# Gate and up projections by Strassen's seven block products, down products in a stage of their own

## The chip, the cores and the metric

The kernel runs on one core of one Trainium2 chip. The metric is the device time of the core in microseconds (us); a single matmul is told in nanoseconds (ns). TensorE does the matmuls, ScalarE (ACT), VectorE (DVE) and GpSimd (POOL) the elementwise work, and SyncE (SP) issues nearly all DMAs. Each engine runs its own instructions strictly in the order in which the program lists them, and engines wait for each other on semaphores.

## The reference

One layer of a streaming encoder on 1152 rows (1024 prompt rows and 8 sample streams of 16 rows), width 1024. Two recurrent mixers come first, then their output product with the residual, then a feed-forward network with a causal convolution of three taps over the rows, which holds most of the arithmetic:

```
x = x + concat(o_gla, o_mlstm) @ w_out
h = rmsnorm(x)                                    # 1152 x 1024
g = h @ w_g ; u = h @ w_u                         # 1024 -> 2816 each
gc = conv_b + sum(conv_w[j] * gp[:, j:j + L] for j in range(3))   # gp: g with the carried rows before it
x = x + (gelu(gc) * u) @ w_d                      # 2816 -> 1024
y = rmsnorm(x)
```

All values are float32. Every large product is made of three matmuls: each operand x is split into a rounded part hi and the rest lo = x - hi, and hi*hi + lo*hi + hi*lo is summed in PSUM.

## The kernel before

The program has three parts that follow each other on every engine: `front` (norm, input projections, GLA mixer), `back` (mLSTM mixer, output product, residual, second norm) and `ffn`. The change leaves `front` as it is.

`back` lists its work once, in `back_order`, and each engine walks that list and does its own share of every item, so an item's place in the list is its place in the queue of each engine. A step s handles 128 rows, in the order `M_STEPS` = 8, 0, 1, ..., 7. Its items are `num` and `um` (recurrence), `turn_b` (hidden rows transposed by TensorE, taken from PSUM by ACT as hi and by DVE as lo), `b` (the second half of the output product, added to the residual rows by DVE, L2041), `sum` (squares on ACT, root on POOL) and `scaled` (ACT scales the 128 rows into `n_rows`, L1755). `turn_n` transposes a block of 384 scaled rows (L1894, 48 transposes) and writes h2T hi (ACT, L1765) and lo (DVE, L2007); the last block of 384 is turned at the head of `ffn` (L2247, 24 transposes). Outputs in PSUM go through a ring of 8 banks: the n-th output waits until the one 8 before it was taken.

`ffn` goes over 11 pairs of 128-wide tiles f of the 2816 columns, nine of the pairs in a hardware loop. For each tile of a pair and each of three blocks of 384 rows (`RBW`) TensorE makes the gate and the up product, 8 parts of the depth by 3 matmuls of 384 columns each (`up`). ACT copies the gate to `gate_prompt` (L2194), DVE does the convolution (L2321, L2324, L2328), ACT the gelu (L2208), DVE multiplies with the up product (L2335), ACT and POOL split the result (L2210, L2161). Then the same pair's down products follow: for 9 row tiles and 2 halves, 2 tiles f by 3 matmuls of 512 columns into bank 6 or 7, added to the residual rows `m_x` in SBUF by DVE (L2341). Weights come in pieces of 128x1024 (512 KB) through three slots, are rounded by ACT (L2172) and their rest made by POOL (L2151). The residual never leaves SBUF. After the last down product DVE and ACT finish the rows (L2232, L2353, L2360) and SP stores them (L2139).

Of the kernel before, what the change touches and what calls it, by code (L numbers as in the profile page):

```python
# [97 lines left out]
class Turn:  # L98

    def __init__(self, nc, sem, name, hT, ident, gain, banks, source, spread=None, eight=None):
        self.spread, self.eight = spread, eight
        self.hT, self.ident, self.gain, self.banks, self.source = hT, ident, gain, banks, source
        self.nb = len(banks)
        self.turned, self.hi_done, self.lo_done = (sem(f"{name}_{n}") for n in ("turned", "hi", "lo"))

    def bank_of(self, rb, k):
        return self.eight[k] if rb == self.spread else self.banks[(rb * KD + k) % self.nb]

    def pe_turn(self, pe, rb, ks=range(KD)):
        for k in ks:
            n = rb * KD + k
            if rb == self.spread:
                if rb and k == 0:
                    pe.wait_ge(self.lo_done, n)
            elif n >= self.nb:
                pe.wait_ge(self.lo_done, n - self.nb + 1)
            for j in range(JR):
                t = pe.transpose(self.bank_of(rb, k)[:, j * P:(j + 1) * P], self.source(rb, j, k), self.ident)  # L120
            t.then_inc(self.turned, 1)

    def act_hi(self, act, rb, ks=range(KD)):
        for k in ks:
            n = rb * KD + k
            act.wait_ge(self.turned, n + 1)
            act.activation(self.hT[0][:, k, rb * RBW:(rb + 1) * RBW], self.bank_of(rb, k)[:, 0:RBW], ACT.Copy,
                           scale=self.gain[:, k:k + 1]).then_inc(self.hi_done, 1)

    def dve_lo(self, dve, rb, ks=range(KD)):  # L130
        for k in ks:
            n = rb * KD + k
            s = slice(rb * RBW, (rb + 1) * RBW)
            dve.wait_ge(self.hi_done, n + 1)
            dve.scalar_tensor_tensor(out=self.hT[1][:, k, s], in0=self.bank_of(rb, k)[:, 0:RBW],
                                     scalar=self.gain[:, k:k + 1], in1=self.hT[0][:, k, s].bitcast(F32),
                                     op0=ALU.mult, op1=ALU.subtract).then_inc(self.lo_done, 1)


class Norm(Turn):  # L140

    def __init__(self, nc, ctx, sem, name, rows, scaled, squares, hT, ident, gain, banks, **spread):
        sb = lambda n, s: ctx.enter_context(nc.sbuf_tensor(f"{name}_{n}", s, F32))
        self.rows, self.scaled_rows, self.squares = rows, scaled, squares
        self.ss = sb("sumsq", [P, RT])
        self.inv = sb("inv", [P, RT])
        self.rstd = sb("rstd", [P, RT])
        self.summed, self.inverted, self.rooted, self.scaled = (  # L150
            sem(f"{name}_{n}") for n in ("summed", "inverted", "rooted", "scaled"))
        super().__init__(nc, sem, name, hT, ident, gain, banks,
                         lambda rb, j, k: scaled(rb * JR + j)[:, k * P:(k + 1) * P], **spread)

    def pe_turn(self, pe, rb, ks=range(KD)):
        if ks[0] == 0:
            pe.wait_ge(self.scaled, rb * JR + JR)
        super().pe_turn(pe, rb, ks)

    def act_sums(self, act, rb, ready, js=range(JR)):  # L160
        for r in (rb * JR + j for j in js):
            ready(act, r)
            if r:
                act.wait_ge(self.summed, r)
            act.activation(self.squares, self.rows(r), ACT.Square,
                           accum_out=self.ss[:, r:r + 1]).then_inc(self.summed, 1)

    def act_root(self, act, rb):
        act.wait_ge(self.inverted, rb + 1)
        s = slice(rb * JR, rb * JR + JR)  # L170
        act.activation(self.rstd[:, s], self.inv[:, s], ACT.Sqrt).then_inc(self.rooted, 1)

    def dve_invert(self, dve, rb, chain):
        s = slice(rb * JR, rb * JR + JR)
        dve.wait_ge(self.summed, rb * JR + JR)
        chain.link(dve.tensor_scalar(self.ss[:, s], self.ss[:, s], 1.0 / D, EPS, ALU.mult, ALU.add))
        dve.reciprocal(self.inv[:, s], self.ss[:, s]).then_inc(self.inverted, 1)

    def dve_scale(self, dve, rb):
        dve.wait_ge(self.rooted, rb + 1)  # L180
        if rb:
            dve.wait_ge(self.turned, rb * KD)
        for j in range(JR):
            r = rb * JR + j
            dve.tensor_scalar(self.scaled_rows(r), self.rows(r), self.rstd[:, r:r + 1], None,
                              ALU.mult).then_inc(self.scaled, 1)
# [2287 lines left out]
```

## Time and profile before

| | us |
|---|---|
| median of 3 runs | 1436.87 (1436.09 to 1437.58) |
| span of the profiled execution | 1438.3 |
| TensorE busy | 1411.8 (98%) |
| VectorE, ScalarE, GpSimd busy | 602.8, 418.9, 469.9 |
| mean DMA rate over the span | 85 GB/s |

The profiled execution's span is 1.4 us above the median of the timed runs. The busy row shows which engine has idle time at all; the view of waits shows who makes TensorE wait; the chain of work that ended last is by its own line TensorE for 94% of the span. In the 40 slices of the page TensorE is at 9 tenths or more in all but the first and the last:

```
PE   7999999999999999999999999999999999999997
DVE  4444132456743455554242433343333333343437
ACT  5341232343323145741212122221212121303123
POOL 5131343457633244432322323232313131313210
```

### The profile page before, as it was taken

How to read it: one execution, taken by the hardware profiler on the slowest of the kernel's cores; microseconds unless marked ns; L12 is line 12 of the kernel's file. 1: busy time of each engine (PE TensorE's matmuls, PEld its weight loads, DVE VectorE, ACT ScalarE, POOL GpSimd, SP SyncE). 2: the span in 40 equal slices, each digit the busy share in tenths (PEclk: the TensorE clock that was granted, in tenths of full speed). 3: DMA queues.
4: the chain of work that ended last, by engine and by line, in shares of the span. 5: the costliest groups of instructions: out<-in, count | busy, mean ns of one | idle time of the engine just before them, and what ended most of it. 6: DMA issues, size and time to landing. Idle time of an engine off the chain costs nothing.

```text
span 1438.3 us, 22509 instructions
## 1 busy us (share of the span) xinstructions
PE 1411.8 (98%) x8739; PEld 1292.4 (90%) x8739; DVE 602.8 (42%) x1234; ACT 418.9 (29%) x889; POOL 469.9 (33%) x452
## 2 busy tenths in 40 slices
PE   7999999999999999999999999999999999999997
PEld 6988888889997788898989899999999999999895
DVE  4444132456743455554242433343333333343437
ACT  5341232343323145741212122221212121303123
POOL 5131343457633244432322323232313131313210
PEclk9999999999999999999999999999999999999999
DMA  6222632335347573121110101010101010111003
GB/s 238 69 79 81 213 121 86 131 108 164 119 137 268 167 218 104 37 90 50 30 59 29 58 29 58 29 58 29 58 27 60 15 54 33 44 43 44 15 21 131
DMA packets 69472, 122.58 MB, mean 85 GB/s; under 512 B 5607, under 2 KB 41219, under 8 KB 68895
## 3 DMA queue, kind: packets, MB, share of 16 engines
q1 hardware_dynamic: 69263, 121.62, 25.4%
q8 instruction: 44, 0.72, 0.2%
q14 instruction: 21, 0.17, 0.0%
q10 hardware_dynamic: 144, 0.07, 0.0%
HBM read 93.02 MB, written 28.64 MB: 85 GB/s over the span
## 4 chain that ended last, share of the span: by engine, by line
PE 94%; DVE 2%; DMA 1%; ACT 1%; POOL 1%; issue 0%; SPq 0%; POOLq 0%; DVEq 0%; ACTq 0%
PE bank L93 29%; PE bank L95 29%; PE bank L94 29%; PE bank L1874 1%; PE bank L1086 1%; PE bank L1143 1%; DVE m_x L2360 1%; PE bank L1827 1%; DMA m_t_in<-scratch_pT 1%; PE bank L1161 1%; PE bank L1857 0%; PE bank L1886 0%; DVE m_x L2341 0%; PE bank L1856 0%; PE bank L1149 0%
## 5 line engine op out<-in xcount | busy, mean ns | idle before, releaser
L93 PE MATMUL bank<-f_h2T_hi,w_hi 128*128 128x384 f32 x1056 | 354.2, 335 | 0.0
L95 PE MATMUL bank<-f_h2T_hi,w_lo 128*128 128x384 f32 x1056 | 353.9, 335 | 0.0
L94 PE MATMUL bank<-f_h2T_lo,w_hi 128*128 128x384 f32 x1056 | 353.5, 335 | 0.0
L2161 POOL TENSOR_TENSOR f_a_lo<-f_gate_conv,f_a_hi 128x384 fp32r<-128x384 f32 x66 | 67.2, 1017 | 574.0 <-ACT f_a_hi L2210 574.0
L93 PEld LDWEIGHTS bank<-f_h2T_hi,w_hi 128*128 128x128 f32 x1056 | 198.3, 188 | 0.4
L94 PEld LDWEIGHTS bank<-f_h2T_lo,w_hi 128*128 128x128 f32 x1056 | 198.2, 188 | 0.4
L95 PEld LDWEIGHTS bank<-f_h2T_hi,w_lo 128*128 128x128 f32 x1056 | 198.2, 188 | 0.0
L2341 DVE TENSOR_TENSOR m_x<-bank,m_x 128x512 f32<-128x512 f32 x198 | 136.9, 692 | 126.1 <-PE bank L95 126.1
L93 PE MATMUL bank<-w_hi,f_a_hi 128*128 128x512 f32 x396 | 154.4, 390 | 0.4 <-DVE m_x L2341 0.2
L95 PE MATMUL bank<-w_hi,f_a_lo 128*128 128x512 f32 x396 | 154.3, 390 | 0.0
L94 PE MATMUL bank<-w_lo,f_a_hi 128*128 128x512 f32 x396 | 154.3, 390 | 0.0
L2321 DVE TENSOR_SCALAR f_gate_conv<-f_gate_prompt,f_taps 128x384 f32<-128x384 f32 (+1 forms) x66 | 35.7, 541 | 271.8 <-ACT f_gate_prompt L2194 179.4
L791 POOL TENSOR_TENSOR w_lo<-w_raw,w_hi 128x1024 fp32r<-128x1024 f32 x33 | 81.1, 2472 | 132.5 <-ACT w_hi L868 132.4
L2194 ACT ACTIVATE f_gate_prompt<-bank 128x384 f32<-128x384 f32 x44 | 21.7, 493 | 331.6 <-PE bank L95 331.6
L93 PE MATMUL bank<-w_hi,p_h1T_hi 128*128 128x512 f32 x288 | 113.0, 392 | 1.0 <-POOL w_lo L791 1.0
L95 PE MATMUL bank<-w_hi,p_h1T_lo 128*128 128x512 f32 x288 | 112.2, 390 | 0.0
L94 PE MATMUL bank<-w_lo,p_h1T_hi 128*128 128x512 f32 x288 | 112.1, 389 | 0.0
L93 PE MATMUL bank<-p_h1T_hi,w_hi 128*128 128x384 f32 x312 | 108.5, 348 | 3.1 <-DVE p_h1T_lo L1219 2.8
L94 PE MATMUL bank<-p_h1T_lo,w_hi 128*128 128x384 f32 x312 | 106.1, 340 | 0.0
L95 PE MATMUL bank<-p_h1T_hi,w_lo 128*128 128x384 f32 x312 | 106.1, 340 | 0.0
L2151 POOL TENSOR_TENSOR w_lo<-w_raw,w_hi 128x1024 fp32r<-128x1024 f32 x42 | 100.5, 2392 | 4.9 <-ACT w_hi L2172 4.9
L93 PEld LDWEIGHTS bank<-w_hi,f_a_hi 128*128 128x128 f32 x396 | 74.3, 188 | 16.8 <-DVE m_x L2341 1.1
(240 smaller groups left out, 2118.7 us busy)
## 6 DMA issues: line engine op xcount, KB each, us to landing
w_raw<-in_w SPq DMA_DIRECT2D x82, 512.0 KB, 3.6
f_raw<-in_w SPq DMA_DIRECT2D x21, 512.0 KB, 3.5
scratch_pN<-p_n_out SPq DMA_DIRECT2D x36, 256.0 KB, 2.1
scratch_pT<-p_t_out SPq DMA_DIRECT2D x36, 192.0 KB, 1.9
p_arena<-in_x SPq DMA_DIRECT2D x9, 512.0 KB, 5.9
p_arena<-scratch_pN SPq DMA_DIRECT2D x18, 256.0 KB, 3.3
m_x<-in_x SPq DMA_DIRECT2D x9, 512.0 KB, 7.9
m_t_in<-scratch_pT SPq DMA_DIRECT2D x9, 512.0 KB, 7.2
```

Of the source, the lines that this page charges most:

```text
L93: pe.matmul(out, stat[0], mov[0], start=start, stop=False)
L94: pe.matmul(out, stat[0], mov[1], start=False, stop=False)
L95: return pe.matmul(out, stat[1], mov[0], start=False, stop=stop)
L791: pool.tensor_tensor(w_lo[:, i % NS_, :], raw[:, i % 2, :], w_hi[:, i % NS_, :].bitcast(F32), ALU.subtract).then_inc(g["piece_split"], 1)
L1086: mm = pe.matmul(out[c * HP:(c + 1) * HP, e, j * 2 * P + at:j * 2 * P + at + QP], half(kx, e)[:, n, j * P + c * HP:j * P + (c + 1) * HP], ...
L1143: mm = pe.matmul(dst(2 * j + e), gsc[:, 2 * j + e, :], vs(2 * j + e), start=True, stop=True, skip_group_check=True)
L1161: mm = pe.matmul(half(out, h)[:, at:at + P], kdn[r, b % 2, j, (h % 2) * DK:(h % 2 + 1) * DK], vin[r, s % 2, h * P:(h + 1) * P], start=True ...
L2151: pool.tensor_tensor(w_lo[:, unit, :], slots[slot], w_hi[:, unit, :].bitcast(F32), ALU.subtract).then_inc(piece_split, 1)
L2161: pool.tensor_tensor(a_lo[q][:, s], gc[:, n % 2, :], a_hi[q][:, s].bitcast(F32), ALU.subtract).then_inc(a_split, 1)
L2194: act.activation(gp[:, 2 + rb * RBW:2 + (rb + 1) * RBW], g[:, 0:RBW], ACT.Copy).then_inc(g_out, 1)
L2321: ins = dve.tensor_scalar(dst, src(2), tap[2], tap[3], ALU.mult, ALU.add)
L2341: dve.tensor_tensor(x, bank[6 + half], x, ALU.add).then_inc(down_added, 1)
```

## The change

The rows are cut into two parts p: rows 0 to 639 as two blocks of 320, rows 640 to 1151 as two blocks of 256. The depth of 1024 and the pair (gate columns, up columns) of a tile f are cut in two as well, and each 2x2 block product is made by seven products in place of eight. One of the seven has a depth of 4 parts, so 4 x 3 = 12 matmuls of 320 or 256 columns. A product needs a sum of weight blocks (a `unit`, 128x512, seven for each f) and a sum of row blocks (a `half`, 4x320 or 4x256 columns on 128 partitions, seven for each p), each split in hi and lo. Outputs accumulate in three PSUM groups, with partial values moved to SBUF in between.

`back` now scales the residual rows in place (after a copy was stored in DRAM, `scratch_res`), transposes them 128 rows at a time (`turn_n`, 8 transposes), and works off the first row and weight sums from its list. `gate_up` makes all products of the 22 tiles without a hardware loop and stores the activations in DRAM (`scratch_act`, 22 x 576 KB). `down` loads them, the down weights and the residual rows again, and makes the down products in 11 chunks of two tiles, with all 8 banks in turn. Matmuls of the down products, their DVE adds and the finishing of the rows keep their number and shape.

```diff
-RBW = 384 row blocks, 24 matmuls of 384 columns for each of gate and up
+NP2 = (320, 256)
+QUADS = 2 * NF
+HALF_POOL = [(0, 0), (0, 1), (0, 2), (1, 0), (1, 1), (1, 4), (1, 5)]
+HALF_DVE = [(0, 3), (0, 4), (0, 5), (0, 6), (1, 2), (1, 3), (1, 6)]
+def quad_order():
+    order = [(0, 0), (0, 1)]
+    for t in range(QUADS):
+        order += [(t, 2), (t, 3), (t, 4)]
+        order += [(t + 1, 0), (t + 1, 1)] if t + 1 < QUADS else []
+        order += [(t, 5), (t, 6)]
...
 back_order, around the last two steps:
+        order += [("turn_n", 4), ("t", 0, 0), ("t", 0, 1), ("half", 0, 0), ("unit", 5)] if s == RT - 1 else []
         order += [("b", s - 2, 1), ("sum", s - 2, 1)] if s >= 2 else take(1)
+        order += {..., 8: [("half", 0, 1), ("unit", 6)]}.get(s, [])
         order += [("b", s - 1, 0)] if s else take(1)
         order += [("sum", s - 1, 0)] if s else []
+        order += {..., 8: [("t", 0, 2), ("scaled", 8), ("scaled", 5), ("half", 0, 2)]}.get(s, [])
+    order += [("b", RT - 2, 1), ("turn_b", RT - 1), ("sum", RT - 2, 1), ("turn_n", 8), ("t", 0, 3)]
+    order += [("b", RT - 1, 0), ("half", 0, 3), ("turn_n", 5), ("b", RT - 1, 1), ("scaled", 6), ("sum", RT - 1, 0), ("sum", RT - 1, 1)]
...
 gate_up, SP:
+        for t in range(QUADS):
+            if t % 2 == 0 and t // 2 + 1 < NF:
+                half.load(sp, a, t // 2 + 1)
+            if t:
+                store(t - 1)
+        store(QUADS - 1)
+        sp.wait_ge(tails_done, 2 * NF)
+        sp.dma_start(o["conv"], tails[:, :, :]).then_inc(tails_out, 16)
 gate_up, ACT (t is a tile f of one part p):
+        for t in range(QUADS):
+            if t:
+                copy_u2(t); copy_p7(t); [keep_tails(f - 1)]; gelu(t - 1); [load_cache(f)]
+            if t == 1:
+                half.hi(act, (1, 5)); half.hi(act, (1, 6))
+            if t + 1 < QUADS:
+                copy_p1(t + 1)           # waits for multiply(t - 1)
+            if t == 0:
+                half.hi(act, (1, 4)); units(7, 8)
+            elif t == 1:
+                units(8, 14)
+            else: units of f + 1: three after p = 0, four after p = 1
+        keep_tails(NF - 1)
+        gelu(QUADS - 1)
 gate_up, DVE:
+        for t in range(QUADS):
+            take_c22(t); [plus(f + 1, 2), plus(f + 1, 3)]
+            take_up1(t + 1); [plus(f + 1, 0), plus(f + 1, 1)]
+            take_c21(t); conv(t)
+            if t == 0:
+                half.lo(dve, (1, 6))
+            multiply(t)
 down, SP, behind all of the above:
+        done.made(sp, last - 1, 3)
+        load_w(0)
+        done.made(sp, last - 1, 5)
+        load_w(1)
+        load_a(0); load_a(1)
+        ... residual rows 0 to 8, then load_w(f), load_a(f) for f = 2 to 21
```

TensorE's waits in `product(t, j)`: j = 2 for `copy_p1(t)`, 4 for `copy_u2(t)`, 5 for `take_c22(t)`, 6 for `copy_p7(t)`, each for its unit (POOL's `unit_lo`), and at f = 0 for its half. The first down matmul waits for the hi and lo of weight tile 0 (ACT, then POOL) and of activation tile 0 (ACT, then DVE).

## Rows read from the trace of the kernel before

**Rows 1.** The page: span and busy time of each engine.

```profile
span 1438.3 us, 22509 instructions
PE 1411.8 (98%) x8739; PEld 1292.4 (90%) x8739; DVE 602.8 (42%) x1234; ACT 418.9 (29%) x889; POOL 469.9 (33%) x452
```

**Rows 2.** Stretches: us, busy by engine, granted clock, DMA share, GB/s.

```profile
5.00:10.00 5.00, 2.08 (x10) 2.12 (x11) 1.51 (x2) 4.28 (x7) 3.11 (x6) 1.00 1.03 408
15.00:20.00 5.00, 5.00 (x16) 5.00 (x17) 3.39 (x7) 4.91 (x9) 1.83 (x2) 0.50 1.00 389
712.00:1400.00 688.00, 688.00 (x3660) 649.74 (x3659) 247.46 (x441) 147.01 (x298) 184.03 (x110) 1.00 0.12 40
```

**Rows 3.** TensorE over time: start us, us, operation; matmul pitch by width.

```profile
567.12 1.05 PE L1827 MATMUL bank<-m_t_in 128*128 128x128 f32 x8
567.93 0.48 PE L93 MATMUL bank<-w_hi,m_mix_b_hi 128*128 128x512 f32 x1
...
577.09 1.47 PE L1894 MATMUL bank<-ident,n_rows 128*128 128x128 f32 x12
578.39 1.06 PE L1827 MATMUL bank<-m_t_in 128*128 128x128 f32 x8
...
603.85 0.33 PE L93 MATMUL bank<-f_h2T_hi,w_hi 128*128 128x384 f32 x1
...
663.44 0.39 PE L93 MATMUL bank<-w_hi,f_a_hi 128*128 128x512 f32 x1
680.44 0.39 PE L93 MATMUL bank<-w_hi,f_a_hi 128*128 128x512 f32 x1
...
1000.04 0.33 PE L93 MATMUL bank<-f_h2T_hi,w_hi 128*128 128x384 f32 x1
1004.20 0.33 PE L93 MATMUL bank<-f_h2T_hi,w_hi 128*128 128x384 f32 x1
...
1428.45 0.39 PE L95 MATMUL bank<-w_hi,f_a_lo 128*128 128x512 f32 x1
```

**Rows 4.** TensorE at the half clock, matmuls of 384 columns.

```profile
18.84 0.52 PE L93 MATMUL bank<-p_h1T_hi,w_hi 128*128 128x384 f32 x1
19.16 0.52 PE L94 MATMUL bank<-p_h1T_lo,w_hi 128*128 128x384 f32 x1
```

**Rows 5.** VectorE, ScalarE, GpSimd groups by shape: busy us, mean ns, idle before.

```profile
L2341 DVE TENSOR_TENSOR m_x<-bank,m_x 128x512 f32<-128x512 f32 x198 | 136.9, 692 | 126.1 <-PE bank L95 126.1
L2324 DVE SCALAR_TENSOR_TENSOR f_gate_conv<-f_gate_prompt,f_taps,f_gate_conv 128x384 f32<-128x384 f32 x44 | 27.2, 618 | 3.8 <-DVE f_gate_conv L2321 2.9
L2360 DVE SCALAR_TENSOR_TENSOR m_x<-m_x,f_rstd,w_raw 128x1024 f32<-128x1024 f32 x9 | 11.4, 1272 | 0.3 <-ACT f_rstd L2224 0.3
L2172 ACT ACTIVATE w_hi<-w_raw 128x1024 fp32r<-128x1024 f32 x42 | 43.9, 1044 | 0.0
L2210 ACT ACTIVATE f_a_hi<-f_gate_conv 128x384 fp32r<-128x384 f32 x66 | 34.7, 526 | 96.5 <-DVE f_gate_conv L2335 96.5
L2151 POOL TENSOR_TENSOR w_lo<-w_raw,w_hi 128x1024 fp32r<-128x1024 f32 x42 | 100.5, 2392 | 4.9 <-ACT w_hi L2172 4.9
L1649 POOL TENSOR_TENSOR m_wt<-m_wt,m_caus 128x512 f32<-128x512 f32 x9 | 11.5, 1280 | 5.3 <-DMA m_wq<-scratch_rows 5.3
```

**Rows 6.** VectorE and GpSimd over time, around 105 us: start us, us, operation.

```profile
104.35 2.54 DVE L1256 TENSOR_TENSOR_SCAN p_arena<-p_arena 4x1152 f32<-4x1152 f32 x1
104.61 4.48 POOL L791 TENSOR_TENSOR w_lo<-w_raw,w_hi 128x1024 fp32r<-128x1024 f32 x1 [4.97 <-ACT w_hi L868]
106.93 3.23 DVE L1258 TENSOR_TENSOR p_arena<-p_arena 4x1024 f32<-4x1024 f32 x1
```

**Rows 7.** From the last output products to the feed-forward part, over time.

```profile
587.76 1.13 DVE L1965 SCALAR_TENSOR_TENSOR m_hidden<-bank,m_den,m_o_in 128x128 f32<-128x128 f32 x4
...
594.69 0.60 PE L1886 MATMUL bank<-ident,m_hidden 128*128 128x128 f32 x4
595.32 0.69 ACT L1793 ACTIVATE m_mix_b_hi<-bank,cols 128x512 fp32r<-128x512 f32 x1
596.05 0.75 DVE L2030 SCALAR_TENSOR_TENSOR m_mix_b_lo<-bank,cols,m_mix_b_hi 128x512 fp32r<-128x512 f32 x1 [0.47 <-ACT m_mix_b_hi L1793]
596.94 0.47 PE L93 MATMUL bank<-w_hi,m_mix_b_hi 128*128 128x512 f32 x1
620.33 1.28 ACT L2208 ACT_TABLE_LOAD   x1
```

**Rows 8.** SyncE's queue at the end of the kernel, over time.

```profile
1374.39 0.34 SPq L2134 DMA_DIRECT2D w_raw<-in_norm_f  x1
1399.93 0.34 SPq L2136 DMA_DIRECT2D out_conv<-f_tails  x1
1413.44 20.59 SPq L2139 DMA_DIRECT2D out_y<-m_x  x9
```

**Rows 9.** DMA issues of the page: KB each, median us from issue to landing.

```profile
w_raw<-in_w SPq DMA_DIRECT2D x82, 512.0 KB, 3.6
p_arena<-in_x SPq DMA_DIRECT2D x9, 512.0 KB, 5.9
```

More of the change, by code:

```diff
@@ L95, in mm3 @@
     return pe.matmul(out, stat[1], mov[0], start=False, stop=stop)
[L98 to L137, printed above, removed]
@@ L140 @@
[L140 to L186, printed above, removed]
@@ L1488, in back_order @@
         order += [("mask", s + 1)] if s + 1 < RT else []
-        order += [("turn_b", s - 1), ("scaled", 3), ("ffn", 0)] if s == RT - 1 else []
+        order += [("turn_b", s - 1), ("unit", 4)] if s == RT - 1 else []
         order += [("num", s)]
@@ L1520, in back_entries @@
         elif x[0] == "turn_n":
-            out += [(("turn_n", x[1], k), "dve") for k in TURN_HALVES[x[2]]]
+            out += [(x + (i,), "dve") for i in range(2)]
         elif x[0] in ("num", "um"):
@@ L1524, in back_entries, with back @@
     return out
-def back(nc, a, o, mem, rows_n, halves_n, early, late, done, ident, cols, col_m, col_d, ssq, ssn, rstd2, power, w, raw, bank,
-         sem, block):
+def back(nc, a, o, mem, early, half, done, ident, cols, col_m, col_d, ssq, ssn, rstd2, power, w, raw, bank, sem, block):
     order = back_order()
@@ L2166, in _ @@
[L2166 removed]
+        for x in HALF_POOL:
+            if x[0] == 1:
+                half.lo(pool, x)
+        for n in range(7, 7 * NF):
+            half.unit_lo(pool, n)
     @block.scalar
     def _(act):
[L2170 to L2178 removed]
@@ new lines, in keep_tails, with units @@
+        def keep_tails(f):
+            act.wait_ge(c21_done, 2 * f + 2)
+            act.activation(tails[:, f, 0:2], gp[:, PROMPT:PROMPT + 2], ACT.Copy).then_inc(tails_done, 1)
+            act.activation(tails[:, f, 2:2 + 2 * NB].rearrange("p (b e) -> p b e", e=2), gs[:, :, LB:SX],
+                           ACT.Copy).then_inc(tails_done, 1)
+        def units(first, end):
+            for n in range(first, min(end, 7 * NF)):
+                half.unit_hi(act, n)
+        half.hi(act, (0, 4))
@@ L2289, in _ @@
-        pairs(pe, body)
+        n = 0
+        for fs in DOWN_CHUNKS:
+            for r in range(RT):
+                for side in range(2):
+                    out = bank[DOWN_BANKS[n % 8]]
+                    if n < 8:
+                        done.bank_free(pe, DOWN_BANKS[n])
+                    else:
+                        added.wait(pe, n - 7)
+                    for f in fs:
+                        if r == 0 and side == 0:
+                            w_split.wait(pe, f + 1)
+                            a_split.wait(pe, f + 1)
+                        mm = mm3(pe, out, [y[:, r * P:(r + 1) * P] for y in rows(f)],
+                                 [y[:, side * 512:(side + 1) * 512] for y in weights(f)], f == fs[0], f == fs[-1])
+                    mm.then_inc(filled.sem, 1)
+                    n += 1
```

1018 lines of the change are left out of this document (655 added, 363 removed).

## The prediction

> **What bounds the kernel now.** I read the page's busy times first: TensorE is busy for 1411.8 of 1438.3 us, no other engine for half of it [rows 1]. The stretches come next. From 712 to 1400 us TensorE is busy for all of 688 us at the full clock [rows 2], so the feed-forward part is bound by the pitch of its matmuls alone. The timeline gives this pitch. From 1000.04 to 1004.20 us there are 24 starts of 384 columns, 173.3 ns each; from 663.44 to 680.44 there are 75 of 512 columns, 226.7 ns each [rows 3]. The difference, 53.4 ns for 128 columns, is 128 cycles of 2.4 GHz, so the pitch is N/2.4 + 13.3 ns. Eight matmuls of 128 columns take 0.81 us, 101 ns each [rows 3], more than the 66.6 ns of that formula: below some width another limit of about 101 to 112 ns takes over (112 if the last of the eight is left out of the count: 1.05 us less the 0.27 of one, over 7). The part from the first gate matmul (603.85) to the last down matmul (1428.45) is 3168 x 173.3 = 549.0 us of gate and up, 1188 x 226.7 = 269.3 of down, 24 transposes of 108 ns (twelve in 1.30 us, same group) = 2.6, and 3.7 us of small stalls.
>
> **What is saved for sure.** Gate and up become 22 x 7 x 12 = 1848 matmuls of 320 and 1848 of 256 columns. By the formula these take 146.7 and 120.0 ns: 271.1 + 221.8 = 492.9 us, 56.1 less than 549.0. The nearest rows from below and above are 128 columns (101 to 112 ns) and 384 (173.3). 256 columns stay above the floor of the first, so I take the line through the two wide rows. If a floor adds to it, 5 ns on the 256-wide ones cost 9 us; I see no way to be faster than the line. The down products stay at 269.3 us. The 72 transposes stay too, 8 of them move ahead of the first product. So TensorE alone would bring 1438.3 - 56.1 = 1382.2 us. The rest of this part is what stands against it, and all of it is idle time of TensorE at three places that the trace of before doesn't have.
>
> A rule on the pitch speaks for a little more: the Trainium skill, page "TensorE: Matmul & The Clock Gate", section "Back-to-back issue gap", gives N/2.4 + 2.5 ns. By it the saving would be 3168 x 162.5 - 1848 x (135.8 + 109.2) ns = 62 us; the trace has 173.3 and not 162.5 ns at 384 columns, and the trace decides.
>
> **Prices of the new elementwise work.** DVE takes 692 ns for 512 columns, 618 for 384 from SBUF, 1272 for 1024: about 1.04 ns a column and 0.2 us; 1280 columns cost 1.5 us, 640 cost 0.9. ACT takes 1.04 us for 1024 and 0.53 for 384, so 1.27 for 1280 and 0.6 for 512. POOL takes 1.28 us for 512 and 2.39 for 1024, so 2.95 for 1280 [rows 5]. One thing more decides: DVE and POOL exclude each other when a DVE instruction has two SBUF inputs. At 104.61 us POOL's split, 2.39 us elsewhere, takes 4.48, since DVE's scan runs until 106.89; then DVE's next operation starts at 106.93 and lasts 3.23 us, until POOL is through at 109.09 and 1.07 us more [rows 6]. They take turns. Nearly all new DVE work (plus, row sums, halves, convolution) has two SBUF inputs. By that row each such operation behind a running POOL one waits for its rest. The Trainium skill has this on the page "SBUF — State Buffer", section "Who interferes with whom": two SBUF inputs on DVE against a GpSimd read lock each other out for whole instructions; this trace agrees.
>
> **Place 1, the last steps of back.** TensorE's b(8,0) needs the last turn_b: in before TensorE ends it at 595.29, ACT and DVE take 0.69 + 0.75 us, and b starts at 596.94 [rows 7]. Now ACT has in front of it, in list order, half (0,0), unit 5, sum (6,1), half (0,1), unit 6, sum (7,0), scaled 8, scaled 5, half (0,2). Sum (6,1) waits for DVE's add b(6,1), which stands behind turn_n 4 (2 x 0.69) and two row sums of 1.5 us, one of them behind POOL's 2.95 us split. I count from the end of hidden(8) on DVE, in before 588.85 [rows 7], now some 1.5 us later behind two weight sums and a turned block, 590.3: states 1.1, turn_n 1.3, sums 3.0, add 0.7 = 596.4. ACT then: 0.7 + 1.27 + 0.6 + 0.7 + 1.14 + 1.14 + 1.27 + 0.7 for turn_b = 603.9, DVE 0.75: b(8,0) starts at 604.9, where TensorE, with 8 more transposes ahead of it than before (0.9 us behind 596.94), is ready at 597.8. That is 7.1 us, and up to 10.8 with POOL's turn in between and its norm chain behind. I take 9.
>
> **Place 2, the first two tiles.** ACT's copy_p1(2) waits for multiply(0). Unit 8, which TensorE's (2,1) needs, stands behind copy_p1(2). From the end of product (0,6): c21 0.5, conv 2.5, table load 1.28 [rows 7], gelu 0.74, halves (1,5) and (1,6) on ACT 2.1, lo (1,6) on DVE 1.3, multiply 0.5, copy 0.45, unit 0.6 + 1.28 = 11.3 us. TensorE has in that time (1,2), (1,3), (1,4) at 1.44 and (2,0) at 1.76 = 6.1. So it idles for 5.2 us at least. DVE is late besides: between (0,4) and conv(0) it has three row sums and three halves of 1.3 to 1.5 us and a fourth sum, while POOL splits three halves of 2.4 us against them. With turns taken I count 10 us more; so 5 to 16, and I take 13.
>
> **Place 3, between gate_up and down.** SP's queue keeps its order: in before norm_f, conv and y leave one after the other, each behind its wait [rows 8]. So load_w(0) stands behind store(43), which waits for the last multiply, although its own wait is long satisfied. After the last gate matmul: c21 0.6, conv 2.5, gelu 0.7, multiply 1.0, so the store leaves at 4.9 us and the first weights at 5.8. A lone piece lands 3.6 us after issue, nine in a burst 5.9 [rows 9], at 408 GB/s [rows 2], 1.3 us for each 512 KB: w0 at 10.4, w1 11.7, a0 13.2, a1 14.6. Then ACT a1 hi to 16.6 and POOL's and DVE's split of w1 and a1 to 19.2, with f = 0's three matmuls done meanwhile: 18.6 us, 15 if the bytes flow better. I take 18. Later loads are covered: a chunk is 108 x 226.7 ns = 24.5 us for 2.2 MB, and eight banks let TensorE run 8 outputs (10.9 us) ahead of DVE.
>
> **The clock.** At 15 to 20 us, after TensorE had waited much, the granted clock was 0.50, 1.2 GHz [rows 2], and 384 columns took 320 ns [rows 4]. Each of the three idle stretches can bring that back: 5 us at half the clock lose about 2.3. I take 6 for three, 0 to 9.
>
> **Steady state and end, costed at nothing.** A tile f takes 12 x 7 x (146.7 + 120.0) = 22.4 us of TensorE. POOL has 7 x 1.28 = 9.0, ACT about 9, DVE about 13, of which 9 exclude POOL. The tightest wait is (t,5) for take_c22(t), behind conv, gelu and multiply of t-1; with POOL's units in between I count it 0.7 to 0.9 us ahead of TensorE. Matmuls, adds and finishing of the last chunk are the same as before.
>
> **The sum.** 1438.3 - 56.1 + 9 + 13 + 18 + 6 = 1428.2 us of span; the timed median lies 1.4 below the span, so 1426.8, rounded to 1427. Low: 7 + 5 + 15 + 0 gives 1407.8. High: 11 + 16 + 20 + 9 gives 1436.8, with 9 us for the 256-wide floor 1446.
>
> **The rivals.** (a) The start is hidden (chance 0.17): ACT and DVE get their work into gaps and places 1 and 2 cost under 10 together, place 3 stays. 1438.3 - 56.1 + 7 + 18 + 2 - 1.4 = 1408. For it speaks that DVE is under half busy [rows 1]; against it, that the waits are in list order. (b) Slower: the turn-taking of DVE and POOL makes take_c22 late in each tile. Price: if conv meets two POOL units of 1.28 us more than I counted, 2.6 - 0.8 = 1.8 us a tile, x 22 = 40, 1467; one in every other part, 0.5 us, 1438. It decides from 0.5 us a tile on. Rows 6 show the mechanism; that my count leaves 0.8 us speaks against it. Chance 0.22. (c) The saving is not as said: a floor of weight loads brings 256 columns to 125 ns, 1436. Chance 0.08. (d) My forecast, 0.53.
>
> **How the numbers follow.** The measurement tells some 0.2%, 2.9 us, from no change: faster is under 1434, slower above 1439.7. Rival (a) and nearly nine tenths of (d) are faster, together 0.63; the rest of (d), most of (c) and the near edge of (b) are within, 0.15; the others are slower, 0.22. The range takes (a)'s middle and cuts off (b)'s far end: 1406 to 1446.
>
> **What would show it.** Pitches of 146 to 148 and 119 to 121 ns in the timeline; gate and up end to end near 493 us plus 13; idle TensorE ahead of b(8,0) behind ACT's m_mix_b hi; ahead of (2,1) behind POOL's unit; ahead of the first down matmul some 18 us behind DMA and the splits, with w_raw's first down load issued after the last store; clock 0.5 after each. I am wrong if TensorE waits for DVE in every tile, or if the three places sum to under 25 or over 55 us.

## The result and the profile after

The changed kernel takes 1433.9 us (median of 17, 1430.42 to 1437.78), the kernel before, measured beside it, 1437.44 (17 runs, 1436.09 to 1442.18). The ratio is 0.9971, 95% interval 0.9962 to 0.9979: 3.5 us faster where I forecast 10. In every one of these runs the span is 1.8 to 1.9 us shorter than the time.

Some lines of the page of the changed kernel; they answer to [rows 1]:

```profile
span 1430.9 us, 23368 instructions
PE 1367.8 (96%) x9267; PEld 1238.5 (87%) x9267; DVE 824.6 (58%) x1463; ACT 470.2 (33%) x967; POOL 538.0 (38%) x503
PE   7999999999999999779999999999999499999997
PEclk9999999999999999898999999999999799999998
```

TensorE is busy 44 us less, not 56, and two dents have come, at slices 17 to 18 and 32. What ended TensorE's waits (total, times, longest):

```profile
PE bank L93 <- DVE d_a_lo L2650: 17.1, 2, 15.3
PE bank L110 <- POOL w_lo L298: 6.8, 1, 6.8
PE bank L330 <- ACT m_x L1710: 3.9, 1, 3.9
PE bank L93 <- DVE m_mix_b_lo L2168: 3.8, 1, 3.8
PE bank L110 <- POOL f_units L298: 2.5, 1, 2.5
PE bank L110 <- ACT f_u L2282: 1.2, 1, 1.2
```

These are the three places of the prediction: place 1 is 3.9 + 3.8 = 7.7 us, place 2 is 6.8 + 2.5 + 1.2 and two waits of 1.0 = 12.5, place 3 is 17.1, 37.3 together against 9 + 13 + 18 = 40. One more wait of 1.0 us, for DVE's take_c22 in the last tile at 1121 us, belongs to none of them. The stretches (busy, count, then granted clock, DMA share, GB/s), which answer to [rows 2]:

```profile
596.00:610.00 14.00, 8.99 (x34) 7.18 (x35) 9.69 (x8) 7.57 (x12) 11.71 (x10) 0.63 0.10 39
640.00:657.00 17.00, 10.82 (x48) 10.48 (x49) 8.84 (x10) 3.66 (x7) 11.50 (x8) 0.60 0.11 34
657.00:1110.00 453.00, 453.00 (x3404) 453.00 (x3404) 300.67 (x490) 160.31 (x366) 187.15 (x140) 1.00 0.22 73
1127.00:1150.00 23.00, 8.66 (x25) 6.50 (x26) 7.38 (x9) 4.85 (x5) 4.92 (x2) 0.56 0.90 343
1200.00:1400.00 200.00, 200.00 (x860) 161.03 (x859) 123.38 (x159) 25.80 (x24) 33.09 (x12) 1.00 0.16 60
```

From 657 to 1110 us TensorE is busy for all of 453.00 us: the steady state has no wait. The clock is 0.56 to 0.63 at the three places and 1.00 in the two long stretches. The last line holds the surprise: 200 us with 860 matmuls of 512 columns are 232.6 ns each, at full clock with TensorE always busy. The timeline of TensorE (start us, us), for the pitches, which answers to [rows 3]:

```profile
699.95 0.29 PE L110 MATMUL bank<-f_b_hi,w_hi 128*128 128x256 f32 x1
701.14 0.28 PE L111 MATMUL bank<-f_t_lo,f_units 128*128 128x256 f32 x1
...
703.49 0.31 PE L110 MATMUL bank<-f_t_hi,w_hi 128*128 128x320 f32 x1
705.40 0.31 PE L111 MATMUL bank<-w_lo,w_hi 128*128 128x320 f32 x1
...
1199.67 0.39 PE L94 MATMUL bank<-w_lo,d_a_hi 128*128 128x512 f32 x1
1201.07 0.39 PE L94 MATMUL bank<-w_lo,d_a_hi 128*128 128x512 f32 x1
```

A step is the time from one start to the next. 10 steps of 256 columns in 1.19 us are 119 ns, 13 of 320 in 1.91 are 147 (forecast 120.0 and 146.7), 6 of 512 in 1.40 are 233.3 ns. In the kernel before the last were 226.7 [rows 3].

Place 1, ScalarE ahead of b(8,0), against [rows 7]. It is ACT's list, as predicted: scaled 5, half (0,2) and turn_b follow each other without a pause.

```profile
598.80 1.15 ACT L1710 ACTIVATE m_x<-m_x,rstd 128x1024 f32<-128x1024 f32 x1 [1.65 <-POOL rstd L1858]
599.86 1.25 ACT L396 ACTIVATE f_t_hi<-ra_k 128x1280 fp32r<-128x1280 f32 x1
601.02 0.67 ACT L1938 ACTIVATE m_mix_b_hi<-bank,cols 128x512 fp32r<-128x512 f32 x1
602.61 0.77 PE L93 MATMUL bank<-w_hi,m_mix_b_hi 128*128 128x512 f32 x1 [3.81 <-DVE m_mix_b_lo L2168]
```

Place 2, TensorE, GpSimd and ScalarE:

```profile
639.01 2.35 POOL L402 TENSOR_TENSOR f_b_lo<-rb_k,f_b_hi 128x1024 fp32r<-128x1024 f32 x1 [5.87 <-ACT f_b_hi L396]
641.31 2.24 POOL L298 TENSOR_TENSOR w_lo<-w_raw,w_hi 128x512 fp32r<-128x512 f32 x1
643.70 0.61 PE L110 MATMUL bank<-f_b_hi,w_hi 128*128 128x320 f32 x1 [6.85 <-POOL w_lo L298]
647.28 0.44 ACT L2266 ACTIVATE f_up<-bank 128x320 f32<-128x320 f32 x1 [7.40 <-PE bank L112]
649.72 0.61 PE L110 MATMUL bank<-f_b_hi,f_units 128*128 128x320 f32 x1 [2.48 <-POOL f_units L298]
```

Here (2,0) is the product j = 0 of t = 2. I had the longest wait one product too late. It is (2,0)'s, for unit 7: POOL splits half (1,5) first, and that half stands behind the first gelu. copy_p1(2) then waits for (2,0) itself, and unit 8 stands behind it. Unit 7 takes 2.24 us, beside a DVE split that runs until 642.43, where the next unit, at 648.31, takes 1.27: the taking of turns of [rows 6], as the Trainium skill's page "SBUF — State Buffer", section "Who interferes with whom", has it.

Place 3, SyncE's queue, which answers to [rows 8], and the first down matmul; w0 is issued 0.8 us behind the last store:

```profile
1128.88 0.32 SPq L2232 DMA_DIRECT2D scratch_act<-c_lo  x1
1129.72 0.94 SPq L2558 DMA_DIRECT2D e_w_lo<-in_w  x2
1139.53 0.77 PE L93 MATMUL bank<-d_w_hi,d_a_hi 128*128 128x512 f32 x1 [15.29 <-DVE d_a_lo L2650]
```

Two profiles are compared best from a point that both have. An a product is the first half of the output product, the matmuls with m_mix_a. The first of back starts at 441.68 us in the profile of before and at 438.78 in that of after, although nothing ahead of it differs; over all fourteen profiles it lies between 438.3 and 442.4. From there to the end before takes 996.6 us, after 992.1. Below, "from the first a product" is this number.

### The profile page after: what moved, and what is told of

It is laid out like the page before. It is cut to its first block, busy times and chain, and to the rows that moved or that the text cites. A ratio compares the mean times of both kernels' runs of the same rounds, so it can differ in the third digit from the quotient of the medians.

```text
span 1430.9 us, 23368 instructions
## 1 busy us (share of the span) xinstructions
PE 1367.8 (96%) x9267; PEld 1238.5 (87%) x9267; DVE 824.6 (58%) x1463; ACT 470.2 (33%) x967; POOL 538.0 (38%) x503
## 3 DMA queue, kind: packets, MB, share of 16 engines
q1 hardware_dynamic: 81359, 157.01, 31.7%
## 4 chain that ended last, share of the span: by engine, by line
PE 90%; DVE 3%; DMA 2%; POOL 2%; ACT 2%; issue 1%; SPq 0%; DVEq 0%; ACTq 0%; POOLq 0%
PE bank L93 17%; PE bank L95 16%; PE bank L94 16%; PE bank L110 11%; PE bank L112 11%; PE bank L111 11%; PE bank L2016 1%; PE bank L1213 1%; PE bank L1270 1%; PE bank L1969 1%; DMA m_t_in<-scratch_pT 1%; PE bank L1288 1%; POOL f_b_lo L402 0%; PE bank L1999 0%; PE bank L1140 0%
## 5 line engine op out<-in xcount | busy, mean ns | idle before, releaser
L2680 DVE TENSOR_TENSOR d_x<-bank,d_x 128x512 f32<-128x512 f32 x198 | 134.8, 688 | 97.3 <-PE bank L95 96.8
L110 PE MATMUL bank<-f_t_hi,w_hi 128*128 128x256 f32 (+1 forms) x412 | 121.3, 294 | 1.2 <-ACT f_u L2282 1.2
L111 PE MATMUL bank<-f_t_lo,w_hi 128*128 128x256 f32 (+1 forms) x412 | 121.1, 294 | 0.0
L112 PE MATMUL bank<-f_t_hi,w_lo 128*128 128x256 f32 (+1 forms) x412 | 121.0, 294 | 0.0
L110 PE MATMUL bank<-f_b_hi,w_hi 128*128 128x320 f32 (+1 forms) x360 | 107.8, 299 | 8.8 <-POOL w_lo L298 6.8
L94 PE MATMUL bank<-w_lo,d_a_hi 128*128 128x512 f32 x288 | 113.9, 395 | 0.0
L95 PE MATMUL bank<-w_hi,d_a_lo 128*128 128x512 f32 x288 | 113.8, 395 | 0.0
L93 PE MATMUL bank<-w_hi,d_a_hi 128*128 128x512 f32 x288 | 113.6, 394 | 0.0
L111 PE MATMUL bank<-f_b_lo,w_hi 128*128 128x320 f32 (+1 forms) x360 | 107.4, 298 | 0.0
L112 PE MATMUL bank<-f_b_hi,w_lo 128*128 128x320 f32 (+1 forms) x360 | 107.4, 298 | 0.0
```

What stands on the lines that cost most here:

```text
L93: pe.matmul(out, stat[0], mov[0], start=start, stop=False)
L94: pe.matmul(out, stat[0], mov[1], start=False, stop=False)
L95: return pe.matmul(out, stat[1], mov[0], start=False, stop=stop)
L110: pe.matmul(out, stat[0], mov[0], start=start, stop=False, skip_group_check=True)
L111: pe.matmul(out, stat[0], mov[1], start=False, stop=False, skip_group_check=True)
L112: return pe.matmul(out, stat[1], mov[0], start=False, stop=stop, skip_group_check=True)
```

## The experiments

Two questions are open: why a down matmul takes 6.5 ns more, and what each of the three places and the clock is worth.

**The pitch: banks and waits, or where the tiles lie.** Four runs. two_banks:

```diff
-DOWN_BANKS = (7, 3, 5, 4, 2, 0, 6, 1)
+DOWN_BANKS = (7, 6) * 4
...
-                        added.wait(pe, n - 7)
+                        added.wait(pe, n - 1)
```

> The changed kernel, but with the down products going in turn to banks 7 and 6 only and each waiting for the add of the output two before, as in the kernel before. In the changed kernel a 512-column matmul of the down stage takes 233.3 ns (232.2 in the chunks of f = 0, 1; 8, 9; 16, 17), in the kernel before 226.8. Theory A (the place of the operands in SBUF: the a tiles begin 320 or 0 bytes past a multiple of 512, the w tiles 352): the pitch stays at 233.3, idle time between outputs stays near 0. Rival B (eight banks in turn, or a TensorE queue that is never held up by a wait, makes the matmuls slower): the pitch falls to 226.8, and the down stage gets 7 us shorter.

Measured: 1451.66 us (one run). The pitch stays; here in the chunk of f = 8, 9, 13 steps in 3.02 us, 232.3 ns (233.1 over the whole stage without the waits):

```profile
1259.96 0.39 PE L95 MATMUL bank<-d_w_hi,d_a_lo 128*128 128x512 f32 x1
1262.98 0.39 PE L93 MATMUL bank<-d_w_hi,d_a_hi 128*128 128x512 f32 x1
```

So B falls. The idle time did not stay near 0, though: with two banks TensorE stops whenever DVE puts a split ahead of an add, 11.8 us in eight waits named for the adds, and 824 matmuls in 200 us instead of 860. The eight banks of the change are worth some 18 us (one run).

all_352:

```diff
-        ("inv", [P, RT], F32), ("rstd", [P, RT], F32), ("gap0", [P, 2632], F32),
-        *a(1), *a(2), *a(3), *a(4), *a(5), ("gap1", [P, 688], F32), *wd(0), *wd(1), *a(0), *a(6), *a(7)])
+        ("inv", [P, RT], F32), ("rstd", [P, RT], F32), ("gap0", [P, 2640], F32),
+        *a(1), *a(2), *a(3), *a(4), *a(5), ("gap1", [P, 768], F32), *wd(0), *wd(1), *a(0), *a(6), *a(7)])
```

> The changed kernel, the down stage's tiles moved so that each begins 352 bytes past a multiple of 512, as w_hi and w_lo do (the a tiles by 32 bytes, w0, w1, a0, a6 and a7 by 352). No instruction differs otherwise. Theory A (SBUF place): 512 columns take 226.7 ns in all eleven chunks, 1188 x 6.4 = 7.6 us less, 1426.3 us against 1433.9 for the changed kernel. Rival B (banks and waits) and rival C (other engines' or DMA traffic in the stage): 233.3 ns, 1434, no change.

Measured: 1425.41 us (1424.64 to 1429.49), ratio to before 0.9927 (0.9913 to 0.994); 984.6 us from the first a product, 7.5 less than after. The stretch from 1200 to 1400 us has 884 matmuls, 226.2 ns each, where after has 860:

```profile
1200.00:1400.00 200.00, 200.00 (x884) 165.68 (x883) 127.68 (x168) 29.50 (x31) 31.76 (x12) 1.00 0.15 57
```

before_320 turns it round, on the kernel before:

```diff
-        *hi_lo("a0", [P, ROWS]), ("raw", [P, PIECE], F32), ("gate_conv", [P, 2, RBW], F32),
+        ("gap4", [P, 8], F32), *hi_lo("a0", [P, ROWS]), ("raw", [P, PIECE], F32), ("gate_conv", [P, 2, RBW], F32),
-        ("taps", [P, NF, 4], F32), ("tails", [P, NF, 2 + 2 * NB], F32), ("gap2", [P, 56], F32),
+        ("taps", [P, NF, 4], F32), ("tails", [P, NF, 2 + 2 * NB], F32), ("gap2", [P, 64], F32),
...
```

> The kernel before, its a0 and a1 tiles (the stationary operand of the down products) moved by 32 bytes, from 352 to 384 past a multiple of 512, the weights left at 352. Theory A: its down matmuls go from 226.8 to about 233.3 ns, 1188 x 6.5 = 7.7 us more, about 1445 against 1437.4, while gate and up stay at 173.3 ns. Rivals B and C: 226.8 ns and no change.

The gaps behind a0 and a1 are 8 smaller, so only raw, gate_conv and four small tiles next to a0 move along, none of them an operand of a matmul. The name of the run says 320, the tiles lie at 384. Measured: 1443.93 us (1442.76 to 1446.59), ratio 1.0046 (1.003 to 1.0061): 6.7 us more. One pair's down stage, 108 matmuls, first and last, 107 steps in 24.96 us, 233.3 ns:

```profile
1183.41 0.39 PE L93 MATMUL bank<-w_hi,f_a_hi 128*128 128x512 f32 x1
1208.37 0.40 PE L95 MATMUL bank<-w_hi,f_a_lo 128*128 128x512 f32 x1
```

part_352 moves a1 to a5 alone (gap0 to 2640, gap1 to 680):

> The changed kernel, only the tiles a1 to a5 of the down stage moved by 32 bytes, to 352 past a multiple of 512; w0, w1, a0, a6 and a7 stay at 0, w_hi and w_lo are at 352. It has all four cases in one run: both at 352 (chunks of f = 2, 3; 4, 5; 10, 11; 12, 13; 18, 19; 20, 21), stationary at 0 with weights at 352 (6, 7; 14, 15), both at 0 (f = 0, 8, 16), stationary at 352 with weights at 0 (f = 1, 9, 17). If the stationary operand's place alone decides: 226.7 ns in the first and the last case, 233 in the other two. If both must be odd multiples of 32 bytes: 226.7 in the first case alone. If they must only agree: 226.7 in the first and the third, which the changed kernel's 232.2 (both at 0 or 320) speaks against.

Measured, step means by chunk: 226.7 to 226.8 ns where both operands lie at 352; 233.4 with the stationary one at 0 and the weights at 352; 231.8 to 231.9 in the chunks that mix both at 0 (f = 0, 8, 16; about 231.6 by themselves) with 352 and 0 (f = 1, 9, 17; about 232.1). The stationary tile's place alone doesn't decide, nor does mere agreement. Of these cases only both at 352 is fast. Time 1428.34 us (one run), 988.2 us from the first a product. The cause of the 6.5 ns is thus shown to be the place of the operands in SBUF; the rule behind it isn't, as the last run but one shows.

**Place 3.** early_down moves four loads (w0, w1, a0, a1), four roundings and two splits ahead of the last two stores, the last gelu and the last convolution:

```diff
...
+            if t == QUADS - 1:
+                start.loads(sp)
             if t:
                 store(t - 1)
...
+        start.his(act)
         keep_tails(NF - 1)
         gelu(QUADS - 1)
...
             take_c21(t)
+            if t == QUADS - 1:
+                start.splits(dve)
             conv(t)
...
```

> The changed kernel; SP issues the loads of w0, w1, a0 and a1 ahead of the stores of the last two tiles, ACT rounds them ahead of the last gelu, DVE splits a0 and a1 ahead of the last convolution. Theory (place 3 is the order of SP's queue): the first down matmul starts about 3 us after the last gate matmul instead of 15.3 and the 1.8 us behind it goes, and with less idle time the half clock of 1127 to 1148 us goes or shortens, 2.6 us more: 14 to 17 us less, about 1418. Rival (the bytes or the splits are the limit whatever the order): the four pieces land about as late after their issue as before, 5 to 7 us, and TensorE still waits 8 us or more, about 1426; or the second chunk comes late (its loads wait for the last store) and TensorE waits there.

Measured: 1431.34 us (1429.3 to 1433.62), ratio 0.9959 (0.9944 to 0.9975), far from 1418. The 17.1 us shrank to 2.9, and a new wait came 20 us later (waits of TensorE, then SyncE's queue, then DVE and ACT ahead of the new wait):

```profile
PE bank L93 <- DVE d_x L2713: 8.8, 1, 8.8
PE bank L93 <- DVE d_a_lo L2560: 2.9, 2, 2.6
...
1135.57 0.32 SPq L2233 DMA_DIRECT2D scratch_act<-c_lo  x1
1136.41 5.08 SPq L2605 DMA_DIRECT2D d_x<-scratch_res  x9
...
1155.69 2.07 DVE L2685 TENSOR_TENSOR d_a_lo<-e_a_lo,d_a_hi 128x1152 fp32r<-128x1152 f32 x1 [11.51 <-ACT d_a_hi L2643]
...
1153.06 1.06 ACT L2641 ACTIVATE w_hi<-c_lo 128x1024 fp32r<-128x1024 f32 x1 [18.31 <-DMA c_lo<-in_w]
```

The residual rows, which DVE adds in the first chunk, still stood behind the last store. The wait bears the name of such an add, but no late row ended it. Rows did hold up DVE's first adds, by 5.3 and 0.75 us. Then DVE stood for 11.5 us in the split of activation tile 2, which its list has ahead of the fifth add. That split waited for ACT, and ACT for weight tile 2, whose load SyncE issued at 1141.66, behind all nine rows. ACT could use it 11.4 us later; the 4.7 MB of rows in front of it take 11 us at the 415 GB/s of the stretch from 1142 to 1153. Eight outputs ahead, TensorE found no free bank. early_x issues these nine loads ahead of the store too (start.loads, and four of them just before the last store):

> As early_down, and the nine loads of the residual rows also go ahead of the last store. In early_down TensorE's wait at the border fell from 17.1 to 2.9 us, but a new one of 8.8 us came at 1149.6 (for DVE's add, itself behind a residual row that landed late, at 374 to 411 GB/s). Theory (bytes in the wrong order: 4.7 MB of residual rows issued only from 1136 us on, with four chunks' pieces behind them): with the rows issued from 1120 us on, both waits are gone, 8 us and part of the half clock less than early_down, about 1421 to 1423. Rival (the DMA rate is the limit, whatever the order): 16 MB have to land between 1118 and 1160 us all the same, TensorE waits for the pieces of f = 2 or 4 instead, and the time stays near 1430.

Measured: 1420.75 us (1419.32 to 1421.94), ratio 0.9883 (0.9866 to 0.9899), the time that the theory had. Waits and queue:

```profile
PE bank L93 <- DVE d_a_lo L2572: 2.6, 1, 2.6
PE bank L93 <- DVE d_x L2715: 1.9, 1, 1.9
...
1119.37 2.86 SPq L2560 DMA_DIRECT2D d_x<-scratch_res  x5
1123.73 2.03 SPq L2560 DMA_DIRECT2D d_x<-scratch_res  x4
```

17.1 us of waits have become 4.5, and 14.5 us are gone from the first a product on. Weight tile 2 is issued at 1140.68, only 1 us sooner than in early_down, but ACT can use it 3.6 us later instead of 11.4. The 1.9 us that are left are the same chain, so the rival was right on the place and wrong on the size.

**Places 1 and 2.** back_order (its first added line stands right behind b(7,0)):

```diff
...
-                  8: [("t", 0, 2), ("scaled", 8), ("scaled", 5), ("half", 0, 2)]}.get(s, [])
-    order += [("b", RT - 2, 1), ("turn_b", RT - 1), ("sum", RT - 2, 1), ("turn_n", 8), ("t", 0, 3)]
-    order += [("b", RT - 1, 0), ("half", 0, 3), ...
+        order += [("b", s - 1, 1), ("turn_b", s), ("half", 0, 1), ("unit", 6)] if s == RT - 1 else []
         order += [("sum", s - 1, 0)] if s else []
...
+                  8: [("scaled", 8), ("t", 0, 2), ("sum", RT - 2, 1), ("scaled", 5), ("half", 0, 2)]}.get(s, [])
+    order += [("b", RT - 1, 0), ("turn_n", 8), ("t", 0, 3)]
+    order += [("half", 0, 3), ...
```

> The changed kernel with the last steps of back in another order: b(7,1) and the last turn_b go ahead of half (0,1), unit 6, scaled 8 and 5, half (0,2); b(8,0) goes ahead of turn_n 8. Theory (place 1 is ACT's list order): ACT's m_mix_b hi starts at about 594 instead of 601.0, b(8,0) at 596 to 599 instead of 602.6, the half clock of 598 to 608 goes, and the first gate product starts 5 to 9 us sooner than 611.5. Rival 1: all of that is kept and the time falls by 5 to 9 us, to about 1426. Rival 2 (the row sums and halves of DVE and POOL are the true limit of the whole start): TensorE waits the same time later, at (1,0) or at place 2, and the time stays within 2 us of 1433.9.

Measured: 1429.72 us (1428.62 to 1432.45), ratio 0.9954 (0.9938 to 0.9971). b(8,0) starts at 596.27 instead of 602.61, the first gate product at 605.20 instead of 611.51, 7.1 us sooner if counted from the first a product. Some of this comes back as waits of 1.49 and 0.29 us for ACT at 608 and 611, and (2,0) is 4.6 us sooner by the same count. From the first a product to the end it takes 987.2 us, 4.9 less than after: between the two rivals. The half clock did not all go: the clock from 590 to 606 us is 0.89.

both_orders adds, on POOL, ACT (behind gelu(0)) and DVE:

```diff
+            if x == (1, 5):
+                half.unit_lo(pool, 7)
             if x[0] == 1:
                 half.lo(pool, x)
...
             if t == 1:
-                half.hi(act, (1, 5))
-                half.hi(act, (1, 6))
+                units(8, 9)
             if t + 1 < QUADS:
                 copy_p1(t + 1)
             if t == 0:
                 half.hi(act, (1, 4))
                 units(7, 8)
+                half.hi(act, (1, 5))
+                half.hi(act, (1, 6))
...
             take_c21(t)
+            if t == 0:
+                half.lo(dve, (1, 6))
             conv(t)
-            if t == 0:
-                half.lo(dve, (1, 6))
             multiply(t)
```

> back_order, and in the first two tiles POOL splits unit 7 ahead of half (1,5); ACT rounds halves (1,5) and (1,6) ahead of the first gelu and unit 8 ahead of copy_p1(2); DVE splits half (1,6) ahead of the first convolution. Theory (place 2 is unit 7 behind half (1,5), which is behind the gelu): the 6.9 us ahead of (2,0) at 643.7 and the 2.5 us ahead of (2,1) fall to 0 to 4 us together, the half clock of 643 to 656 goes, 3 to 4 us more: 8 to 12 us less than back_order. Rival (DVE and POOL are busy to the brim there and take turns): the wait only moves to another product, 0 to 3 us less.

Measured: 1423.24 us (1422.74 to 1427.81), ratio 0.9914 (0.9896 to 0.9931), 982.5 us from the first a product, 4.7 less than back_order (by the medians 6.5). The wait ahead of (2,0) is gone; the one ahead of (2,1) has grown from 2.5 to 4.8 us, for unit 8 behind the gelu. That is under my 8 to 12, and the clock from 636 to 653 us is still 0.80.

**The clock.** kept_busy takes no wait away, but keeps TensorE at work in it (of its five additions, the one at the border):

```diff
...
+        for k in range(115):
+            pe.transpose(bank[7][:, 0:P], ident, ident)
```

> The changed kernel; while TensorE waits at the three places it transposes the identity into a bank that the next product overwrites: 30 times ahead of turn_n 8, 28 ahead of b(8,0), 50 and 12 ahead of (2,0) and (2,1), 115 ahead of the first down matmul, each 0.11 us at full clock, a little less than each wait. No wait is taken away. Theory (the clock's price stands beside the idle time's): no stretch at 1.2 GHz behind the three places, the waits end when they did, and the matmuls that were slow there (in the changed kernel 24 at 0.43 us at place 1, some 25 at the start of (2,0), 10 at the border) run at full pitch: 7 to 9 us less, 1425 to 1427 against 1433.9. Rival (the half clock costs little, since the engines that TensorE waits for set the pace of those stretches anyway): 0 to 3 us less, above 1431.

Measured: 1428.65 us (1426.32 to 1431.9), ratio 0.9938 (0.9925 to 0.9951); 986.1 from the first a product, 6.0 less. The stretches of the three places:

```profile
596.00:612.00 16.00, 13.98 (x93) 12.21 (x92) 11.78 (x11) 8.44 (x15) 11.99 (x11) 1.00 0.09 35
640.00:657.00 17.00, 14.56 (x107) 14.08 (x106) 12.02 (x20) 5.41 (x13) 9.73 (x7) 1.00 0.25 81
1122.00:1145.00 23.00, 18.20 (x111) 15.68 (x110) 7.66 (x8) 4.22 (x4) 4.94 (x2) 0.85 0.95 363
```

At places 1 and 2 the clock is 1.00 instead of 0.63 and 0.60, and nearly all of the 6 us is there: the first down matmul starts 5.5 us sooner. At place 3 the 115 transposes ended 3.0 us too soon and the first matmuls were again at 1.2 GHz. In the changed kernel the border's slow matmuls (12, most of them at 0.43 us instead of 0.23) cost 2.5 us; here 9 of them are left, 2.0 us.

**All together.** all_orders is all_352, both_orders and early_x in one:

> The changed kernel with the down tiles at 352, both new orders at the start, and the loads, roundings and splits of the first down chunk and the residual rows ahead of the last store. If the gains are independent, they add: against the kernel before the ratios were 0.9971 for the changed kernel, 0.9927 (down tiles), 0.9914 (both orders), 0.9883 (early loads): 1 - 0.0029 - 0.0044 - 0.0057 - 0.0088 = 0.9782, 1406 us; by the medians 8.5 + 10.7 + 13.2 = 32 us, 1401.5. Theory: 1401 to 1407. Rival (a faster start or border makes the DMA or DVE the limit behind it): over 1411.

Measured: 1401.16 us (1399.36 to 1405.07), ratio 0.9744 (0.9728 to 0.9761). From the first a product it takes 961.3 us, 30.8 less than after; the three parts give 7.5 + 9.7 + 14.5 = 31.7. They add, within 1 us: this version beats both kernels, by 32.7 and 36.4 us.

mix_unit8 (in back_memory gap0 312 to 304, gap1 384 to 392; on ACT `units(8, 9)` ahead of `gelu(0)`):

> all_orders with two more edits: the tiles of back from t_in to C_prompt moved down by 32 bytes, so that mix_a, the stationary operand of the a products, begins 288 instead of 320 past a multiple of 512; and ACT rounds unit 8 ahead of the first gelu. In the kernel before 216 matmuls with mix_a take 233.2 ns and those with mix_b (at 352) 226.7. Theory A: 288 and 352 are both odd multiples of 32, so the a products go to 226.7 to 227 ns, 216 x 6.5 = 1.4 us less; if the place must be the same as that of the weights modulo 512, they stay at 233. Unit 8: TensorE's 4.8 us ahead of (2,1) fall to about 1.8, since DVE's split of half (1,6) ends 3 us before the gelu can start, and part of the half clock behind goes. Together 3 to 5 us less than 1401.2: 1396 to 1398. Rival: the wait moves to (2,2), whose unit needs DVE's sums of the new tile behind multiply(0): 0 to 2 us.

Measured: 1401.15 us (1398.16 to 1403.43), ratio 0.9732 (0.971 to 0.9754), no gain that can be told. The first a product's step goes from 233.3 ns (in all_orders 2.80 us for 12) to 229.2 (2.75 us), neither of the two values I had named: an odd multiple of 32 bytes is not the whole rule. (The b products with w, whose operands didn't move, went from 230 to 231 ns at the same time. They stand at the head of their product, where the first seven or eight steps take up to 236 ns before they settle at 227; the steps compared here are settled ones.) Unit 8's wait falls from 4.8 to 0.9 us, and 2.0 us come back at once ahead of (1,5), which waits for DVE's take_c22, and 1.3 more in the turns ahead. That is the rival in kind, though it had named (2,2). At the border 2.5 us come too, at 1136, by the chain of early_down.

mix_kept adds 10, 15, 18 and 18 transposes:

> mix_unit8, and TensorE transposes the identity while it waits: 10 times ahead of turn_n 8, 15 ahead of b(8,0), 18 ahead of (2,1), 18 ahead of the first down matmul. Theory (the clock's price): in all_orders the granted clock was still 0.89 to 0.85 in the stretches of the three places; with it at 1.00, 2 to 3 us less than mix_unit8, about 1394. Rival: the transposes delay the work themselves or the half clock comes all the same: within 1 us of mix_unit8.

Measured: 1400.73 us (1400.05 to 1402.97), ratio 0.9737 (0.9718 to 0.9756), the same. The clock was 1.00 at places 1 and 2, as in the first line, and from 1108 to 1120 us. The other lines are 20 us into the down stage (SyncE's queue, DVE, TensorE, and the stretch from 1120 to 1125 us):

```profile
640.00:660.00 20.00, 18.85 (x144) 18.82 (x144) 17.15 (x23) 7.58 (x17) 11.29 (x8) 1.00 0.23 83
...
1125.22 0.33 SPq L2630 DMA_DIRECT2D c_lo<-in_w  x1
...
1131.61 2.11 DVE L2706 TENSOR_TENSOR d_a_lo<-e_a_lo,d_a_hi 128x1152 fp32r<-128x1152 f32 x1 [9.96 <-ACT d_a_hi L2664]
...
1134.37 0.80 PE L93 MATMUL bank<-d_w_hi,d_a_hi 128*128 128x512 f32 x1 [3.01 <-DVE d_x L2734]
...
1120.00:1125.00 5.00, 5.00 (x24) 4.14 (x23) 1.65 (x3) 0.00 (x0) 0.00 (x0) 1.00 0.37 141
```

TensorE began the down stage sooner (at 1114.2 instead of 1117.1) and waited 3.0 us at 1134. The name is again that of DVE's add, the chain again that of early_down: DVE stood for 10 us in the split of activation tile 2, behind ACT, behind weight tile 2. SyncE issued that load at 1125.22, after it had waited 4.5 us for the last store to land, while the DMA share was 0.37. So what is in the way here is first of all the order of the queue, not the bytes: the loads of the second chunk still stand behind the last store. Whether they can go ahead of it was not tried. Behind this wait, from 1134 to 1145 us, the clock was 0.71, so the border's price came back in another place.

## Why the prediction was off

- **Gate and up, -56.1 us:** right. The pitches came out at 119.2 and 146.7 ns, so 3696 matmuls take 491.4 us, 57.6 less. The gap of 13.3 ns that the line through two widths gave holds at 320 columns, and at 256 within 1 ns; the 2.5 ns that the Trainium skill's page "TensorE: Matmul & The Clock Gate", section "Back-to-back issue gap", gives for an isolated matmul do not show here. Rivals (b), DVE late in every tile, and (c), a floor at 256, fell: no wait in 453 us, 119 ns.
- **The three places, 40 us:** right in size (37.3) and in mechanism, but for place 2, where the longest wait is (2,0)'s for unit 7; that its sum still met 13 is in part luck. The new orders and loads gave 4.9, 4.7 and 14.5 us from the first a product, with their share of the clock. At places 1 and 2 that is not all: waits of 3.5 and 8.7 us stay there in both_orders.
- **The clock, 6 us:** too low. 6.0 us came back in kept_busy (by the medians 5.3), nearly all at places 1 and 2, and 2.0 more stayed at the border: 8.0.
- **"The down products stay at 269.3 us", the step that failed.** They take 1188 x 233 = 277 us, 7.5 more. The time came 6.9 us above the forecast; what the other terms are off by (-1.5, -2.7, +1.0 and +2.0 us) nearly cancels. I had read the pitch from a stage whose tiles lay elsewhere and taken the width of the matmul for all that sets it. The new memory list was in the diff. A warning stood in the trace of before as well, at the same width and with weights at 352 too. These are the starts of two neighbouring a products and of two b products:

```profile
441.68 0.40 PE L93 MATMUL bank<-w_hi,m_mix_a_hi 128*128 128x512 f32 x1
444.48 0.39 PE L93 MATMUL bank<-w_hi,m_mix_a_hi 128*128 128x512 f32 x1
...
589.25 0.39 PE L93 MATMUL bank<-w_hi,m_mix_b_hi 128*128 128x512 f32 x1
591.97 0.39 PE L93 MATMUL bank<-w_hi,m_mix_b_hi 128*128 128x512 f32 x1
```

  Twelve matmuls take 2.80 us (233.3 ns) with mix_a, at 320, and 2.72 (226.7) with mix_b, at 352. I read only the like of the second. all_352 takes 7.5 us away by moving tiles and lands at 1425.4, near the forecast 1427.
- **The sum, from the first a product:** -57.6 + 37.3 + 8.0 + 7.5 = -4.8; the 1.0 us at 1121 comes to it, and a wait of 0.8 us that before has at 457 and after has not goes: -4.6. Measured 992.1 - 996.6 = -4.5. That leaves no room for another large term; the small stalls of both kernels I took as equal. The medians say 3.5, within what one profiled run differs from another.
- **From span to time:** I took the timed median 1.4 us below the span of the profile. In the runs of the result the time is 1.8 us above the span, so the profiled execution of before was some 3 us longer than its median. The forecast of the difference does not hang on it.

## What to carry to other kernels

Before a pitch is carried to a stage whose tiles move, look where both operands of the matmul will lie; other places for the tiles gave 7.5 us here, the two new orders at the start 9.7, and the tiles cost two numbers in a list. Where a stage border idles, move every transfer that the next stage needs ahead of the last store, those of its second user too: with four of thirteen moved, early_down got 3 us, with all of them early_x got 13. A wait that bears the name of an add need not be the add's own: look at what the engine did before it. And price an idle stretch with the slow matmuls behind it: here 37 us of idle time cost 8 more.
